# Eight of twelve parts of a conditioning product move from TensorE matmuls to row-wise sums on VectorE

## The reference, cut to what matters

```
mod = silu(c) @ w_ada + b_ada          # (1024) @ (1024, 6144)
sh_m, sc_m, gt_m, sh_f, sc_f, gt_f = split(mod, 6)
h = rms_norm(x, g_pre_mix) * (1 + sc_m) + sh_m
x = x + gt_m * rms_norm(mixing(h), g_post_mix)
h = rms_norm(x, g_pre_ffn) * (1 + sc_f) + sh_f
x = x + gt_f * rms_norm(moe(h), g_post_ffn)
```

## Time and profile before

| | us |
|---|---|
| median of 3 runs | 1566.22 (1560.23 to 1566.35) |
| the profiled execution, its own time | 1566.34 |
| its span in the trace | 1564.5 |
| TensorE busy | 1374.2 (88%) |
| VectorE busy | 592.3 (38%) |
| ScalarE busy | 325.5 (21%) |
| GpSimd busy | 186.9 (12%) |

### The profile page before, as it was taken

One profiled execution on the slowest core, in us unless ns is written; L12 is line 12 of the kernel. 1 busy time (PEld: TensorE's weight loads), 2 busy tenths in 40 slices (PEclk: granted clock), 3 DMA queues, 4 the chain that ended last, 5 costly groups with the idle time before them and its releaser, 6 DMA issues.

```text
span 1564.5 us, 44960 instructions
## 1 busy us (share of the span) xinstructions
PE 1374.2 (88%) x18685; PEld 792.8 (51%) x18686; DVE 592.3 (38%) x1648; ACT 325.5 (21%) x843; POOL 186.9 (12%) x267
## 2 busy tenths in 40 slices
PE   3999998998897599999998997799988999997974
PEld 1446454555554255555555554455545555554542
DVE  2203332666446334343343342324333343342325
ACT  1111000565522011112121111111111212111113
POOL 4000000344300101001010010001000001010031
PEclk8899999898897699999999998999999999998998
DMA  9744712700064979999999999999999799999993
GB/s 332 257 145 160 270 68 103 300 1 1 1 260 171 410 314 426 425 427 415 425 427 425 423 426 426 426 418 425 425 426 424 309 398 428 424 426 425 426 409 112
DMA packets 77064, 506.00 MB, mean 323 GB/s; under 512 B 9320, under 2 KB 15952, under 8 KB 52448
## 3 DMA queue, kind: packets, MB, share of 16 engines
q1 hardware_dynamic: 66624, 474.96, 73.8%
q0 software_dynamic: 6560, 20.00, 3.3%
q10 hardware_dynamic: 3840, 10.49, 1.8%
HBM read 473.89 MB, written 31.52 MB: 323 GB/s over the span
## 4 chain that ended last, share of the span: by engine, by line
PE 63%; DMA 27%; DVE 5%; issue 2%; ACT 1%; SPq 1%; DVEq 0%; ACTq 0%
DMA arena<-in_w_down 26%; PE ps L1741 23%; PE ps L1761 13%; PE ps L1411 10%; PE ps L1663 4%; PE ps L1532 2%; PE ps L1594 2%; PE ps L1555 2%; PE ps L1359 1%; DMA arena<-in_w_ada 1%; DVE arena L1035 1%; ACT arena L708 1%; PE ps L1749 1%; DVE arena L1307 1%; PE ps L1581 1%
## 5 line engine op out<-in xcount | busy, mean ns | idle before, releaser
L1741 PE MATMUL ps<-arena 128*32 128x256 f32 x10240 | 594.0, 385 | 55.4 <-issue 31.4
L1741 PEld LDWEIGHTS ps<-arena 128*32 128x32 f32 x10240 | 344.8, 112 | 282.0 <-issue 65.1
L1761 PE MATMUL ps<-arena 128*32 128x256 f32 x5120 | 311.4, 395 | 46.5 <-DMA arena<-in_w_down 46.1
L1276 DVE TENSOR_SCALAR arena<-ps 128x128 f32<-128x128 f32 x160 | 46.8, 292 | 600.1 <-PE ps L1749 595.1
L1761 PEld LDWEIGHTS ps<-arena 128*32 128x32 f32 x5120 | 158.9, 112 | 175.3 <-issue 62.0
L782 ACT ACTIVATE arena<-ps 32x256 f32<-32x256 f32 x320 | 120.1, 375 | 334.6 <-PE ps L1761 301.0
L1411 PE MATMUL ps<-arena 128*128 128x512 f32 (+1 forms) x384 | 161.2, 575 | 0.9 <-DVE arena L877 0.9
L776 ACT ACTIVATE arena<-arena 128x128 f32<-128x128 f32 x160 | 49.7, 311 | 523.0 <-DVE arena L1276 523.0
L574 POOL DMA_INDIRECT arena<-xn_rows,arena x81 | 78.5, 969 | 388.9 <-DVE arena L1246 388.3
L1411 PEld LDWEIGHTS ps<-arena 128*128 128x128 f32 x384 | 73.2, 195 | 81.3 <-issue 76.0
L561 POOL TENSOR_SCALAR arena<-arena 128x128 f32<-128x128 f32 (+3 forms) x48 | 52.0, 1083 | 329.8 <-DVE arena L1057 295.0
(11 more groups left out here) (317 smaller groups left out, 933.4 us busy)
## 6 DMA issues: line engine op xcount, KB each, us to landing
arena<-in_w_up SPq DMA_DIRECT2D x128, 2048.0 KB
arena<-in_w_down SPq DMA_DIRECT2D x64, 2048.0 KB, 29.2
arena<-in_w_ada SPq DMA_DIRECT2D x12, 2048.0 KB, 11.5
slot_rows<-arena SPq DMA_DIRECT2D x4, 3328.0 KB, 25.3
arena<-in_w_in SPq DMA_DIRECT2D x5, 2048.0 KB, 7.7
slot_rows<-arena ACTq DMA_DIRECT2D x80, 128.0 KB, 6.2
arena<-in_w_o SPq DMA_DIRECT2D x2, 2048.0 KB, 9.0
arena<-in_x SPq DMA_DIRECT2D x4, 512.0 KB, 15.0
```

What stands on the lines that cost most here:

```text
L1741: ins = pe.matmul(out_of(y, g), xgT[:, 2 * n + k, :], tiles[par][n][:, k, at:at + 256], start=(n == 0 and k == 0), stop=False)
L1761: ins = pe.matmul(out_of(5, g), actT[:, y, k, :], tiles[par][4 + y][:, k, 256 * g:256 * (g + 1)], start=False, stop=(y == 1 and k == 3))
```

## The change

For parts 4 to 11 TensorE's eight matmuls go. VectorE computes the part itself: with weights laid out as partition p, j = 0 to 7, 512 columns (input feature 8p + j), it multiplies `w[:, 0, :]` by the scalar `silu(c)[8p]`, and adds `w[:, j, :]` times `silu(c)[8p + j]` for j = 1 to 7 into the same row, each instruction linked to the one before. The row then holds 128 partial sums per column, and the turn adds all 128 partitions with a column of ones in place of the selecting column. `row_sb`, set by the last of the eight instructions, gives the ring slot back for these parts. The activated vector stays in a tile of its own, `c_act`, that nothing overwrites. Parts 0 to 3 are as before, and so are the order of the ring and VectorE's order of rows and evacuations. On TensorE the parts are gone from between the blocks, and the turns stand behind later blocks than before; the first projection also waits for the constants of GpSimd.

```diff
--- before.py
+++ after.py
@@ -176,6 +176,7 @@
         ab2 = put(16)
         ctab = put(3 * N_PART + 1, parts=1, dt=I32)
         fin = put(20)
+        c_act = fin[:, 0:KT]
         biasw = put(4, D // 4, dt=BF16)
         gidx_all, slot_i, gk = put(MAX_CH, dt=I32), put(16, dt=I32), put(NT, TOP_K)
         idxg = put(1, dt=I32)
@@ -359,6 +360,7 @@
         UP_ORDER = [(0, 0), (1, 0), (0, 1), (1, 1), (0, 2), (0, 3), (1, 2), (1, 3)]
         TILE_H, TILE_2 = 0, 8
         BCONST = 13
+        PE_ADA = 4
 
         block = ctx.enter_context(nc.Block())
 
@@ -391,7 +393,7 @@
             def slot_used(n):
 
                 kind, m = RING[n][0]
-                done, count = {"ada": (ada_ps, m + 1), "in": (pj_ps, NT * (m + 1)), "c1": (hid_u, 1),
+                done, count = {"ada": (ada_ps if m < PE_ADA else row_sb, m + 1), "in": (pj_ps, NT * (m + 1)), "c1": (hid_u, 1),
                                "wo": (wo_ps, 2 * (2 * NT - 1 + m))}[kind]
                 sp.wait_ge(done, count)
 
@@ -837,18 +839,32 @@
             v.wait_ge(silu_e, 1)
             link(v.tensor_scalar(ctmp[:, 1, :], ctmp[:, 0, :], 1.0, None, ALU.add))
             link(v.reciprocal(ctmp[:, 2, :], ctmp[:, 1, :]))
-            link(v.tensor_tensor(cvec, cvec, ctmp[:, 2, :], ALU.mult))
-            v.tensor_copy(silu_c, bc(cvec, 2, 32)).then_inc(silu_ready, 1)
+            link(v.tensor_tensor(c_act, cvec, ctmp[:, 2, :], ALU.mult))
+            v.tensor_copy(silu_c, bc(c_act, 2, 32)).then_inc(silu_ready, 1)
 
             v.wait_ge(vt_ps, 1)
             link(v.tensor_copy(vt, ps[:, 7, 0:88]))
             v.tensor_copy(posT, ps[:, 7, 128:144]).then_inc(vt_sb, 1)
 
             def ada_rows(n):
-                v.wait_ge(ada_ps, n + 1)
                 if n >= 2:
                     v.wait_ge(modc_ps, n - 1)
-                v.tensor_copy(mrow[:, n % 2, :], ps[:, 2, :]).then_inc(row_sb, 1)
+                row = mrow[:, n % 2, :]
+                if n < PE_ADA:
+                    v.wait_ge(ada_ps, n + 1)
+                    v.tensor_copy(row, ps[:, 2, :]).then_inc(row_sb, 1)
+                    return
+                at = at_ring[("ada", n)]
+                v.wait_ge(ring_in[RING[at][1]], 16 * (len(before_in_slot(at)) + 1))
+                w = ring_view(at)
+                link(v.tensor_scalar(row, w[:, 0, :], c_act[:, 0:1], None, ALU.mult))
+                for j in range(1, KT):
+                    ins = v.scalar_tensor_tensor(out=row, in0=w[:, j, :], scalar=c_act[:, j:j + 1], in1=row,
+                                                 op0=ALU.mult, op1=ALU.add)
+                    if j < KT - 1:
+                        link(ins)
+                    else:
+                        ins.then_inc(row_sb, 1)
 
             def ada_cols(lo, hi):
                 v.wait_ge(modc_ps, hi)
@@ -1362,15 +1378,16 @@
 
             def ada_t(n):
                 pe.wait_ge(row_sb, n + 1)
+                total = const(C_SEL4, 1) if n < PE_ADA else ones_f[:, 0:1]
                 if 6 <= n < 10:
                     at, rows = (24, 32)[n // 8], slice(64 * (n % 2), 64 * (n % 2) + 64)
                     for j in range(KT):
-                        ins = pe.matmul(ps[rows, 3, at + j:at + j + 1], mrow[:, n % 2, j:512:KT], const(C_SEL4, 1),
+                        ins = pe.matmul(ps[rows, 3, at + j:at + j + 1], mrow[:, n % 2, j:512:KT], total,
                                         start=True, stop=True)
                 else:
                     for q in range(4):
                         ins = pe.matmul(ps[:, 3, 4 * n + q:4 * n + q + 1], mrow[:, n % 2, q * P:(q + 1) * P],
-                                        const(C_SEL4, 1), start=True, stop=True)
+                                        total, start=True, stop=True)
                 ins.then_inc(modc_ps, 1)
 
             def turn_tiles(base, src, ready, count, strided=False, part=range(KT)):
@@ -1414,13 +1431,6 @@
                     if i in between:
                         between[i]()
 
-            def with_ada(n):
-
-                def second():
-                    ada_t(n)
-                    ada(n + 1)
-                return {0: lambda: ada(n), 1: second, 2: lambda: ada_t(n + 1)}
-
             def turn_group(g):
                 kind, j = GROUPS[g]
                 if g >= 4:
@@ -1479,16 +1489,17 @@
                                         start=(j == 0), stop=(j == 1))
                 ins.then_inc(cv_ps, 1)
 
-            project(0, with_ada(4))
-            project(1, with_ada(6))
+            pe.wait_ge(bconst, BCONST)
+            project(0, {3: lambda: ada_t(4)})
+            project(1, {0: lambda: ada_t(5), 1: lambda: ada_t(6), 3: lambda: ada_t(7)})
             pe.wait_ge(pj_ev, PJ[0] + NT)
             turn_groups(0, 4)
-            project(2, with_ada(8))
+            project(2, {2: lambda: ada_t(8), 3: lambda: ada_t(9)})
             pe.wait_ge(roped, 1)
             turn_groups(4, 8)
             pe.wait_ge(roped, 2)
             turn_groups(8, 14)
-            project(3, with_ada(10))
+            project(3, {2: lambda: ada_t(10), 3: lambda: ada_t(11)})
             pe.wait_ge(roped, 3)
             turn_groups(14, 16)
             project(4, {0: lambda: gain_product(0, (row_sb, 12)), 1: hidden, 2: hidden_turned, 3: compressed})
```

## The result

The changed kernel takes 1551.16 us (median of 5 runs, 1547.68 to 1555.0), the kernel before 1566.22 beside it (5 runs, 1560.23 to 1566.65): ratio 0.9926, 95% interval 0.9904 to 0.9949, 15.1 us faster. The forecast was 1550.5. The profiled execution took 1551.16 us.

A forecast was written before the change was run, and what follows sets the result against it. TensorE, 63% of the chain and 99% busy in the projections, was taken to bound the kernel; 14.8 us of parts plus 0.9 of back-to-back blocks took 1566.34 to 1550.6, forecast 1550.5 us, range 1549.5 to 1552 (60%).

The forecast's parts named there:

- TensorE's parts are on the chain: Between projection blocks on TensorE: removing the matmuls of parts 4 to 11, eight at 1.85 us each, saves 14.8 us.
- Blocks back to back: In the projections: a 512-wide block behind the same kind takes 6.92 us, not 7.06; 0.9 us saved in all.
- A part is 5.8 us on VectorE: Between 50.6 and 188.6 us: one product and seven linked multiply-adds take 5.8 us a part, 46 us in all.
- the line: VectorE times at 512 columns, interpolated between 128 and 1024 columns: 718 ns for a multiply-add, 483 ns for a product.
- The rows are ready in time: In projections 0 to 3: VectorE finishes each row before its turn on TensorE; turn 8 is tightest, 0.7 us to spare.
- VectorE's late rows as a rival: At turns 8, 9 and 11: slower multiply-adds or part 9's late load make TensorE wait, up to 1558.5 us; chance 14%.
- The threshold: At turns 8 and 9: TensorE waits once a part takes 6.2 us on VectorE, 2 us for each us more.
- The clock: Last block of projection 2: one fall to 1.2 GHz stays, 5.66 us for 3.97; rival that it goes, 1548.8 us, 12%.
- the prediction's own signs of being wrong: TensorE waiting at turn 8 or 9, multiply-adds above 0.78 us, clock 0.5 in projections 1 or 3, longer stages after 261 us.
- The sum of 15.7 us: Through projection 3: 14.8 us of parts and 0.9 us of blocks back to back, moving its end from 188.62 to 172.9 us.
- The Trainium skill's rule: On TensorE: activity releases the throttle, so a busy engine stays at 2.4 GHz; by it alone 1548.8 us; the prediction kept 5.66.
- The shift reaches the end: Behind the projections: nothing is tied to a fixed time, so the first stage's shift reaches the end one to one.

## Why the prediction was right

- *TensorE's parts are on the chain, 14.8 us.* Shown: put back, they cost 15.2 us (2.2 more than their removal gained on that chip, which stays open); half of them gives half of the gain.
- *Blocks back to back, 0.9 us.* As forecast in size: the chain has 29.72 us for projection 0 and 20.60 for three blocks of projection 3.
- *A part is 5.8 us on VectorE.* It is 5.92 (121.08 to 127.00). The multiply-add took 752 ns for 718 on the line; the product 486 for 483. The line between two sizes was 5% low for the multiply-add; the 35 ns from one instruction to the next held.
- *The rows are ready in time, turn 8 the tightest at 0.7 us.* Row 8 was 1.5 us early. The other rows ended within two microseconds of where the text had them; part 7's load did set the start of its row.
- *VectorE's late rows as a rival.* The threshold was not tried; but at 11.4 us a part the loss was 16.8 us, where the prediction's 2 us for each above 6.2 gives 10.4. It left out the load of part 6, which row 5 sets free (4.3 us at turn 6), and had turns 8, 9 and 11 wait less than the 12.1 us measured. The rival was undersized.
- *The clock.* This step was off, and a granted clock of 0.5 in projection 1, one of the prediction's own signs of being wrong, was there. The sum carried over one dip; the trace of the changed kernel has three, and with the slow transposes projections 1 and 2 took 34.4 and 21.6 us in place of 32.9 and 21.0, the groups 3.0 in place of 1.75. In all, the stretch was 125.2 us, not 122.3. Against that, the first block began at 48.82 and not at 50.64 us, since work before the projection ran at 2.4 GHz, which the kernel before did at 1.2 (one of its parts 0 to 3 and the turn behind it took 2.96 and 1.87 us, now 1.92 and 1.05); and 0.96 us came from behind projection 3. The traces of all kernels have the first block between 48.0 and 51.4 us, so this is not of the change. The sum of 15.7 us against 15.6 measured in the span thus agrees better than its terms: 2.9 us too few for the stretch were made good by 1.8 and 0.96 us that the sum did not have. The mechanism was right; that the number came within 0.7 us was partly luck, as the executions of the changed kernel lie 5 to 13 us apart on one chip and the two repeats give 13 us. The 2 to 3 us missing there have the size of two dips more at 1.7 us each, which is an estimate and not shown for the medians.
- *The Trainium skill's rule*, TensorE: Matmul & The Clock Gate, section "What's actually happening" (activity releases the throttle), would have had no dip in a TensorE that is always busy. The rows at 98, 114 and 132 us contradict that here.
- *The shift reaches the end.* Shown: the transposes behind the last projection begin at 246.00 and not at 260.58 us, 14.6 earlier, and what follows projection 3 took 1375.9 us before and 1374.9 after, in the two traces.

## What to carry to other kernels

Where the chain runs through one engine back to back, time taken off that engine is gained nearly one to one (13 to 15 us of 15.7 here), as long as each replacement is ready in the order of its own engine's queue; lay both orders out in time before believing it. A freed buffer must be given back by the new, early reader: with the same work, the late give-back cost 19 to 22 us. A margin found by such a layout is worth only as much as the layout's list of waits; a load that can start only when the slower row is done belongs in it.

## What the runs showed of the hardware

- TensorE's clock fell to 1.2 GHz for some 3.4 us while it was busy without a break: in 16 of 25 cases behind a 2.01 us turn of sixteen one-column matmul records, in none of 7 where a part followed the turn. Each fall that lay in the blocks cost 1.7 us (5.66 us in place of 3.97, 15.63 in place of 13.93).
- A weight load of columns with a step of eight words is slow: 217 ns for 64 and 335 for 128 columns, against 138 and 192 side by side.
- A float32 multiply-add of 128x512 in SBUF takes 752 ns in order and about 1110 ns, with a step of 64 words as with one of 128, when its output and the input that it adds to are walked with such a step.
- The same kernel took 1566.2, 1563.9, 1555.0 and 1555.7 us in four measurements, the last three on three different chips: 0.7% between the ends, as much as this change brings.
